# A hybrid linear-attention and sliding-window layer on one core: query/key projection by channels, and three sets of PE transposes given to DMA transposes

## What is computed

```python
h = rmsnorm(x, g_pre) * (1 + scale) + shift
gq, gk, gv, gg, ga, sq, sk, sv, sg = split(h @ w_in)
# linear attention (GLA): 4 heads, dk 64, dv 128, a forget gate per channel
log_a = log_sigmoid(ga @ w_alpha + b_alpha) / 16
S_t = exp(log_a) * S_(t-1) + k_t^T v_t ;  o_gla = (q_t * 64**-0.5) S_t
o_gla = rmsnorm(o_gla, gla_norm_g) * silu(gg)
# sliding window (SWA): 8 query heads, 2 key heads, hd 64, chunks of 64 tokens,
# own chunk and the one before, partial rotary, a learned sink per head
o_swa = sink_attention(rope(sq), rope(sk), sv) * silu(sg)
y = x + gate * rmsnorm(concat(o_gla, o_swa) @ w_out, g_post)
```

## Time and profile before

| | before |
| --- | --- |
| median of 3 runs | 1677.62 us |
| profiled run | 1677.3 us |
| its span, first to last instruction | 1675.6 us |
| busy PE, DVE, ACT, POOL | 1604.8, 1001.4, 659.0, 413.8 us |
| PE busy in a tile of 46.65 us in the middle | 46.65 us |
| mean granted PE clock | 0.979 |
| DMA, mean over the span | 71 GB/s |

### The profile page before, as it was taken

The page is one execution under the profiler, slowest core; times in us unless marked ns, Lnnn a source line. Parts: engine busy times, 40 slices in busy tenths (PEclk is TensorE's granted clock), DMA queues, the critical chain, the costliest instruction groups (busy, mean ns, idle before and its releaser), DMA issues.

```text
span 1675.6 us, 30638 instructions
## 1 busy us (share of the span) xinstructions
PE 1604.8 (96%) x12203; PEld 947.3 (57%) x12203; DVE 1001.4 (60%) x1711; ACT 659.0 (39%) x1983; POOL 413.8 (25%) x439
## 2 busy tenths in 40 slices
PE   8277999999999999999999999999999999999996
PEld 3135665555666666565566666556566666655553
DVE  1257665556666666655666666655656666655554
ACT  0254443443443434443444344444343433434432
POOL 0111222222222222222222222222222222222221
PEclk9679999999999999999999999999999999999998
DMA  8944322111122222121212222212112222221302
GB/s 271 296 120 102 90 64 64 50 50 38 50 63 63 63 63 63 56 57 37 51 50 63 63 63 63 63 50 51 37 55 58 63 63 63 63 63 45 79 18 61
DMA packets 199047, 119.13 MB, mean 71 GB/s; under 512 B 147005, under 2 KB 186438, under 8 KB 199014
## 3 DMA queue, kind: packets, MB, share of 16 engines
q1 hardware_dynamic: 189574, 115.51, 25.1%
q10 hardware_dynamic: 9440, 3.17, 0.9%
HBM read 49.23 MB, written 17.59 MB: 40 GB/s over the span
## 4 chain that ended last, share of the span: by engine, by line
PE 89%; DVE 2%; issue 1%; DMA 1%; ACT 1%; POOL 0%; ACTq 0%; SPq 0%; POOLq 0%
PE bank L446 55%; PE pairP L446 21%; PE pairQ L629 2%; PE bank L539 2%; PE bank L535 2%; PE bank L559 2%; PE pairP L582 1%; PE pairQ L546 1%; PE pairQ L603 1%; PE bank L570 1%; DMA hT<-h_tok 1%; PE bank L596 1%; PE bank L641 1%; PE pairQ L607 0%; PE bank L637 0%
## 5 line engine op out<-in xcount | busy, mean ns | idle before, releaser
L446 PE MATMUL bank<-w_hi,hT 128*128 128x512 f16 (+1 forms) x2640 | 751.1, 361 | 30.9 <-DMA hT<-h_tok 30.8
L446 PE MATMUL bank<-w_lo,hT 128*128 128x512 f16 (+1 forms) x1320 | 475.9, 361 | 0.0
L446 PEld LDWEIGHTS bank<-w_hi,hT 128*128 128x128 f16 x2640 | 259.0, 98 | 288.5 <-DMA hT<-h_tok 31.1
L446 PE MATMUL pairP<-wo_hi,late 128*128 128x512 f16 x1056 | 321.7, 381 | 2.5 <-DVE late L1025 2.5
L446 PE MATMUL pairP<-wo_lo,late 128*128 128x512 f16 x528 | 201.2, 381 | 0.0
L446 PEld LDWEIGHTS bank<-w_lo,hT 128*128 128x128 f16 x1320 | 129.7, 98 | 114.7 <-issue 1.9
L446 PE MATMUL bank<-hT,w_hi 128*128 128x128 f16 x2112 | 183.5, 221 | 3.2 <-DVE w_lo L913 3.2
L446 PE MATMUL bank<-hT,w_lo 128*128 128x128 f16 x1056 | 181.1, 221 | 0.0
L446 PEld LDWEIGHTS pairP<-wo_hi,late 128*128 128x128 f16 x1056 | 104.0, 99 | 125.0 <-DVE late L1025 2.9
L1172 POOL TENSOR_TENSOR xs<-xs,shift_row 128x1024 f32<-128x1024 f32 x33 | 79.7, 2414 | 374.2 <-DVE xs L929 374.2
L446 PEld LDWEIGHTS bank<-hT,w_hi 128*128 128x128 f16 x2112 | 162.7, 99 | 5.4 <-issue 3.3
(11 more groups left out here) (212 smaller groups left out, 2250.0 us busy)
## 6 DMA issues: line engine op xcount, KB each, us to landing
x_res<-x_in SPq DMA_DIRECT2D x33, 512.0 KB, 3.5
x_in<-in_x_prompt SPq DMA_DIRECT2D x32, 512.0 KB, 3.1
out<-stage SPq DMA_DIRECT2D x32, 512.0 KB, 2.7
w_hi<-in_w_ada SPq DMA_DIRECT2D x5, 1024.0 KB, 9.3
w_lo<-in_w_ada SPq DMA_DIRECT2D x5, 1024.0 KB, 13.1
wo_lo<-in_w_in SPq DMA_DIRECT2D x5, 1024.0 KB, 11.8
wo_hi<-in_w_in SPq DMA_DIRECT2D x3, 1024.0 KB, 11.2
stage<-in_w_ada SPq DMA_DIRECT2D x2, 1024.0 KB, 11.6
```

The costliest lines, as they stand in the source:

```text
L446: last = pe.matmul(out, a(c, i), b(c, j), start=(c == 0 and n == 0), stop=(c == KC - 1 and n == 2))
```

## The change

Three things are changed. The QK projection is made by channels, like the sg projection: four outputs [128 channels, 128 tokens], 24 matmuls each with 128 moving columns, so ACT's copy to `etmp` and the four transposes of line 570 are gone; DVE's products read bank4 directly and descale there. The mixed GLA rows are split in token-major form, high half by ACT and low half by DVE, into `m_tok`, which lies in the first half of `xs`; SP turns them by one DMA transpose into `mixT`, whose order is now slice, then half; the four transposes of line 582 are gone, and `x_scaled` waits for the transpose. The q and k pairs are turned by three DMA transposes (`transpose_qk`: two of 64 partitions for q, one for k straight into `kB`), issued by SP in every tile but tile 0, where ACT issues them; the twelve transposes of lines 603 and 607, ACT's copy to `qT` and DVE's copies from PSUM are gone, DVE copies half of `kB` into `kA` after the products with the decay. New waits: PE's output projection on `mT_loaded`, PE's scores on `qT_loaded`, SP on `mg_lo` and `pair_lo`, ACT on `mix_gla` ahead of its copies of the key and value projection.

```diff
@@ -146,11 +146,12 @@
...
         swa_ch = lambda a: a.rearrange("p (j k) -> p j k", j=KC // 2)
-        mixT = late[:, D:2 * D].bitcast(F16).rearrange("p (s c k) -> p s c k", s=2, c=KC)
+        mixT = late[:, D:2 * D].bitcast(F16).rearrange("p (c s k) -> p c s k", s=2, c=KC)
         x_in = sb("x_in", [P, 2, D])
...
         xs = sb("xs", [P, D])
+        m_tok = xs[:, 0:GH * DV].bitcast(F16).rearrange("p (c s k) -> p c s k", s=2, c=GH)
         hT = sb("hT", [P, 2, 2, KC, P], F16)
@@ -160,6 +161,7 @@
...
         qT = sb("qT", [P, 2, HEADS, CHUNK], F16)
+        q_tok_hb = qk_tok[:, 0:4, :].rearrange("p b (g k) -> p g b k", g=KVH)
         kA = sb("kA", [P, KVH, 2, P], F16)
@@ -170,12 +172,11 @@
...
         etmp = sb("etmp", [P, 512])
-        q_pair = etmp[:, :].bitcast(F16).rearrange("p (h s k) -> p h s k", h=HEADS, s=2)
+        q_pair = etmp[:, :].bitcast(F16).rearrange("p (g b s k) -> p g b s k", g=KVH, b=4, s=2)
         cache_k_tok = x_res[0:CHUNK, 0:P]
...
         cache_rows = cache_k_tok.rearrange("p (h k) -> p h k", h=KVH).unsqueeze(2).to_broadcast([CHUNK, KVH, 2, HD])
-        heads_tok = qk_tok[:, :, :].rearrange("p b (g k) -> p (b g) k", g=2)
-        k_twice = heads_tok[:, 8:10, :].unsqueeze(2).to_broadcast([P, KVH, 2, HD])
+        k_twice = qk_tok[:, 4, :].rearrange("p (g k) -> p g k", g=2).unsqueeze(2).to_broadcast([P, KVH, 2, HD])
         lsp = sb("lsp", [P, 2, P])
@@ -241,9 +242,6 @@
...
         gaT_ps = bank5[:, :].bitcast(F16)[0:2 * LOWRANK, 0:P]
-        pair16 = pairQ[:, :].bitcast(F16)
-        q_pair_ps = pair16[:, 0:HEADS * P].rearrange("p (h k) -> p h k", h=HEADS)
-        k_pair_ps = pair16[:, HEADS * P:(HEADS + 4) * P].rearrange("p (h s k) -> p h s k", h=KVH, s=2)
         cache_ps = bank4[:, :].bitcast(F16)[:, 0:4 * CHUNK].rearrange("p (h s k) -> p h s k", h=KVH, s=2)
...
@@ -273,6 +271,8 @@
...
         hT_loaded = [ctx.enter_context(nc.semaphore(f"hT_loaded{i}")) for i in range(2)]
+        mT_loaded = ctx.enter_context(nc.semaphore("mT_loaded"))
+        qT_loaded = ctx.enter_context(nc.semaphore("qT_loaded"))
         pT_loaded = ctx.enter_context(nc.semaphore("pT_loaded"))
@@ -301,6 +301,14 @@
...
             return w[:, :, at:at + HD]
+
+        def transpose_qk(eng):
+
+            for ch in range(2):
+                eng.dma_start_transpose(qT[:, ch, :, :], q_pair[CHUNK * ch:CHUNK * (ch + 1)].rearrange("p g b s k -> p (g b s k)"))\
+                   .then_inc(qT_loaded, 16)
+            eng.dma_start_transpose(kB[:, :, :, :].rearrange("p g s k -> p (g s) k"),
+                                    k_pair.rearrange("p g s d k -> p (g s d k)")).then_inc(qT_loaded, 16)
 
@@ -383,6 +391,19 @@
...
                         sp.dma_start(row_chunks(row[:, :]), mod_row(n, 1)).then_inc(scale_loaded[1], 16)
+                if c.prev:
+                    sp.wait_ge(sem["mg_lo"], c.t)
+                    sp.wait_ge(sem["pv_mm"], c.t)
+                    sp.wait_ge(pT_loaded, 16)
+                    sp.sem_inc(sem["mT_go"], 1)
+                    sp.dma_start_transpose(mixT[:, 0:GH, :, :].rearrange("p c s k -> p (c s) k"),
+                                           m_tok.rearrange("p c s k -> p (c s k)")).then_inc(mT_loaded, 16)
+                if c.cur and not c.first:
+                    sp.wait_ge(sem["pair_lo"], c.t + 1)
+                    sp.wait_ge(sem["ka_prev"], c.t + 1)
+                    sp.wait_ge(pT_loaded, 16)
+                    sp.sem_inc(sem["qT_go"], 1)
+                    transpose_qk(sp)
                 if c.next and not c.first:
@@ -513,13 +534,22 @@
...
 
+                def project_channels(out, first, done):
+
+                    for b in range(4):
+                        col = first + P * b
+                        last = split_product(out[:, b, :], lambda cc, i: (w_hi, w_lo)[i][:, cc, col:col + P], h)
+                    last.then_inc(done, 1)
+
                 if c.cur:
...
                         pe.wait_ge(sem["at_d"], t)
-                    project(bank4, 512, W_QK, sem["qk_mm"])
+                    if c.first:
+                        pe.wait_ge(w_split, in_units_before[W_QK])
+                    project_channels(qk_ch, W_QK, sem["qk_mm"])
                     if c.first:
@@ -565,22 +595,9 @@
...
                     project(bank7, 512, W_SQ, sem["sq_mm"])
-                    pe.wait_ge(sem["qk_ev"], t + 1)
-                    for b in range(4):
-                        last = pe.transpose(qk_ch[:, b, :], etmp[:, b * P:(b + 1) * P], ident[:, :])
-                    last.then_inc(sem["qkt_mm"], 1)
                     pe.wait_ge(sem["ksg_ev"], t + 1)
...
                     pe.transpose(gaT_ps, ga_pair[:, :], ident16[:, :]).then_inc(sem["gat_mm"], 1)
-                if c.prev:
-                    pe.wait_ge(sem["mix_gla"], t)
-                    if c.second:
-                        pe.wait_ge(sem["modt_ev"], 2)
-                    else:
-                        pe.wait_ge(sem["y_mul"], t - 1)
-                    for cc in range(GH):
-                        last = pe.transpose(pairP_c[:, cc, :], gates[:, cc * P:(cc + 1) * P], ident[:, :])
-                    last.then_inc(sem["mixt_mm"], 1)
                 if c.cur:
@@ -596,22 +613,17 @@
...
                     last.then_inc(sem["z_mm"], 1)
-                    pe.wait_ge(sem["pair_lo"], t + 1)
-                    if c.prev:
-                        pe.wait_ge(sem["s_upd"], t)
-                    for head in range(HEADS):
-                        last = pe.transpose(q_pair_ps[:, head, :], q_pair[:, 2 * (head % 4) + head // 4, :, :],
-                                            ident16[:, :])
-                    for g in range(KVH):
-                        for part in range(2):
-                            last = pe.transpose(k_pair_ps[:, g, part, :], k_pair[:, g, part, :, :], ident16[:, :])
-                    last.then_inc(sem["qks_mm"], 1)
                 if c.prev:
                     pe.wait_ge(sem["mixt_lo"], t)
+                    pe.wait_ge(mT_loaded, 16 * t)
+                    if c.second:
+                        pe.wait_ge(sem["modt_ev"], 2)
+                    else:
+                        pe.wait_ge(sem["y_mul"], t - 1)
                     for n in range(2):
...
                             pe.wait_ge(w_split, len(IN_UNITS) + (n + 1) * OUT_UNITS // 2)
-                        last = split_product(pairP[:, 512 * n:512 * (n + 1)], lambda cc, i: mixT[:, i, cc, :],
+                        last = split_product(pairP[:, 512 * n:512 * (n + 1)], lambda cc, i: mixT[:, cc, i, :],
                                              lambda cc, i: (wo_hi, wo_lo)[i][:, cc, 512 * n:512 * (n + 1)])
@@ -619,8 +631,10 @@
...
                     mod_to_rows(2 * KC, 3 * KC, 2)
-                pe.wait_ge(sem["qks_ev"], t + 1)
+                pe.wait_ge(qT_loaded, 48 * (t + 1))
                 pe.wait_ge(sem["k_ev"], t + 1)
+                if c.prev:
+                    pe.wait_ge(sem["s_upd"], t)
                 for ch in range(2):
@@ -646,10 +660,7 @@
...
                     pe.wait_ge(w_split, in_units_before[W_SG])
-                for j in range(KC // 2):
-                    col = W_SG + P * j
-                    last = split_product(bank6[:, P * j:P * (j + 1)], lambda cc, i: (w_hi, w_lo)[i][:, cc, col:col + P], h)
-                last.then_inc(sem["sg_mm"], 1)
+                project_channels(swa_ch(bank6[:, :]), W_SG, sem["sg_mm"])
 
@@ -750,12 +761,15 @@
...
                     rsqrt_of(o_r[:, :], o_ln[:, :], o_ss[:, :], DV, sem["o_lnd"], sem["o_rs"], t)
+                if c.prev:
+                    act.wait_ge(sem["mix_gla"], t)
+                    act.activation(m_tok[:, :, 0, :], swa_ch(gates[:, 0:512]), ACT.Copy).then_inc(sem["mg_hi"], 1)
                 if c.cur:
...
                     if c.prev:
-                        act.wait_ge(sem["qks_mm"], t)
+                        act.wait_ge(qT_loaded, 48 * t)
                     if c.sample:
@@ -766,10 +780,6 @@
...
                        .then_inc(sem["ksg_ev"], 1)
-                    if c.prev:
-                        act.wait_ge(sem["sg_g"], t)
-                    act.wait_ge(sem["qk_mm"], t + 1)
-                    act.activation(etmp[:, :], bank4[:, :], ACT.Copy, scale=DESCALE).then_inc(sem["qk_ev"], 1)
                     act.wait_ge(sem["sq_mm"], t + 1)
@@ -785,14 +795,14 @@
...
                 if c.prev:
-                    act.wait_ge(sem["mixt_mm"], t)
-                    act.activation(mixT[:, 0, 0:GH, :], pairP_c[:, 0:GH, :], ACT.Copy)
                     act.wait_ge(sem["mix_swa"], t)
-                    act.activation(mixT[:, 0, GH:KC, :], swa_ch(gates[:, 512:1024]), ACT.Copy).then_inc(sem["mixt_hi"], 1)
+                    act.activation(mixT[:, GH:KC, 0, :], swa_ch(gates[:, 512:1024]), ACT.Copy).then_inc(sem["mixt_hi"], 1)
                 if c.cur:
                     act.wait_ge(sem["rope"], t + 1)
-                    act.wait_ge(sem["qkt_mm"], t + 1)
```

(39 more changed lines are left out.)

6 lines of the change are left out of this document (3 added, 3 removed).

## The result

The changed kernel is slower: 1761.49 us median (4 runs, 1757.87 to 1761.87) against 1677.57 for the kernel before, a ratio of 1.0493 (95% interval 1.0479 to 1.0507). The forecast was 1643.4, range 1630 to 1655. The profiled execution took 1757.87 us; its span is 1756.1, 80.5 more than before.

A forecast was written before the change was run, and what follows sets the result against it. The prediction took TensorE (PE) as the limit in steady tiles, 46.72 us each. Profiled run 1677.3 - 46.8 (31 tiles x 1.51) + 12.6 for first and last tiles = 1643.1, set to the median: 1643.4 us, range 1630 to 1655.

The forecast's parts named there:

- The steady tile: Tiles 2 to 32: PE work removed less work added saves 1.51 us a tile (1.42 to 1.68), 46.8 us over 31.
- The QK exchange: QK projection: four f32 transposes go (0.44 us), 96 matmuls of 128 columns replace 24 of 512 (0.29 us dearer).
- the removal of the other sixteen transposes: PE, steady tile: transposes of GLA rows (0.59 us), q pairs (0.55) and k pairs (0.22) leave the chain.
- The transfers hide in steady tiles: Steady tiles: new DMA transposes land before PE needs them, GLA rows over 6 us spare, q/k 5; cost nothing.
- late copies: Rival, 5%: the copy into kA comes late by about a microsecond in every tile; 1675 us.
- transposes in series: Rival, 5%: the three q/k transposes land one after the other, 4.2 us each, 2.0 us stall a tile; 1706 us.
- the exchange: Rival, 2%: QK's 96 matmuls cost 69 ns each, 6.6 us, leaving 0.4 us gain a tile; 1678 us.
- The ends: First two tiles and last one: new waits cost 12.6 us in all (8 to 17).
- Tile 0: ACT's three q/k transpose issues delay the squares of the next x to 119.4: +4.3 us (2.5 to 6.8).
- Tile 1: Output projection waits for the GLA transpose queued on SP, then runs at a lower clock: +7.1 us (5 to 8.5).
- the last tile: Tile 33: output projection waits for the low half and the transpose's landing: +1.2 us (0.5 to 1.9).
- PE's loop body no longer stays on the engine: Rival, 3%: PE's grown loop is fetched at each of 14 turns, 4.2 us each, 59 us; 1702 us.

The follow-up runs named there:

- experiment 3: Changed kernel with the QK projection token-major again (ACT's copy and four f32 transposes back), DMA transposes kept: 1654.07 us.
- Experiment 1: Changed kernel with PE's loop written out, all 34 tiles one behind the other without a jump back (the written-out kernel): 1649.69 us.
- the edit that undoes the order: Written-out changed kernel, with ACT issuing tile 0's q/k transposes behind its decay exponentials instead of ahead of the next x's squares: 1643.12 us.
- experiment 5: Kernel before with the channel-major QK projection only, plus 24 PE transposes (48 instructions) into an unused bank ahead of tile 0: 1730.54 us.
- the kernel with 78 transposes: Changed kernel, loop kept, with 78 PE transposes (156 instructions) into an unused bank ahead of tile 0: 1726.22 us.
- both kernels with one wait a jump: The kernel of experiment 5 (1730.54 us) and the kernel with 78 transposes (1726.22 us).
- all eight kernels with a loop: Before; token-major QK; channel QK alone, also with 24 transposes; changed, also with 48, 78, or 12 transposes and two first-tile edits: 1640.6 to 1761.5 us.

## Why the prediction was wrong

**The steady tile was right in kind, a tenth too large in size.** Forecast 1.51 us a tile (1.42 to 1.68), measured 46.72 - 45.37 = 1.35, below the lower bound. The QK exchange alone gave 0.20 where the step had 0.44 - 0.29 = 0.15; 57 ns a matmul held: half of the 10.83 us piece is 5.41. Too large was the removal of the other sixteen transposes: 1.14 by experiment 3, not 1.36. The chain shows the 0.22: the V projection, which now follows one single transpose, takes 5.29 where it took 5.18 behind the transposes of line 582, and the output projection 10.47 behind the decay matmuls where it took 10.36 behind line 607. The V projection in the chain of before, right behind line 582:

```profile
817.92 5.18 PE bank L446 x24
```

So each of these two pieces costs 0.11 us more without the transposes in front of it: what a transpose takes in the chain is not all given back when it goes. Why is not shown; four decay matmuls in front don't do the same. With the 0.05 that the exchange gave beyond its step, 1.51 - 1.35 = 0.16 is missing in a tile, 5.0 us over 31.

**The transfers hide in steady tiles: right.** SP's issues in the changed kernel, in the tile without the stop, and DVE's copy into kA:

```profile
913.43 1.24 SPq L399 DMA_TRANSPOSE late<-xs  x1
923.75 2.51 SPq L308 DMA_TRANSPOSE qT<-etmp  x2
926.31 1.26 SPq L310 DMA_TRANSPOSE kB<-junk  x1
933.68 1.84 SPq L413 DMA_TRANSPOSE hT<-h_tok  x1
```

```profile
929.03 1.93 DVE L1093 COPY kA<-kB 128x256 f16<-128x256 f16 x1
```

POOL's addition of the shift at that time, and the landing of the GLA rows (median):

```profile
928.52 2.35 POOL L1186 TENSOR_TENSOR xs<-xs,shift_row 128x1024 f32<-128x1024 f32 x1 [7.19 <-DVE xs L940]
```

```profile
late<-xs SPq DMA_TRANSPOSE x33, 2.7
```

The small transposes issue in 1.24 to 1.26 us each (forecast 1.14 and 0.79, bounds 0.43 and 1.85); by the trace's list of DMA issues they land in 2.5 to 2.7 us, not 3.5. The GLA rows are there by 916.1, PE takes them at 923.84; kA is ready at 930.96 and the scores begin at 934.31, 3.4 us later, where 5 were forecast at the middle price. Not the landing took the difference but the copy: the step put it at 0.2 us, and it took 1.93, where a copy of the same shape at line 1054 takes 0.22. It ended 0.09 us behind POOL's addition of the shift. In all 32 tiles with that addition the copy takes 1.06 to 1.94 and ends 0.07 to 0.09 behind it; in tile 32, which has none, it takes 0.23. So the copy is held until POOL is done, and the step had no such term. Experiment 1 settles it: 45.37 us in each tile, without the time that the jumps gave. So the rivals "late copies" and "transposes in series" fall, and with 5.41 us for 96 matmuls "the exchange" too.

**The ends: 14.3 us at the start, not 11.4, and 0.1 at the end, not 1.2** (0.1 is the -1.3 above and the 1.35 of one tile, which the forecast counts among its 31). Tile 0: the squares at 119.92, forecast 119.4 (a shift of 4.81, forecast 4.3); the edit that undoes the order starts them at 113.59, 6.53 sooner than in the written-out kernel, and gave 6.6: the chain held, one for one. Tile 1: the output projection started at 182.02, forecast 179.2. The step took SP's queue as shifted by tile 0's 4.3; x_res was issued at 174.31, 7.3 later than before, because the output weights ahead of it had slipped as well (SP's last issue for them at 171.32, 164.06 before), and the load of x behind it waited for its copy. The forecast had the right instruction in front of the transpose and didn't follow what delays that one. The projection took 12.55 - 11.09 = 1.46 longer, forecast 1.6, at a granted clock of 0.84 against 0.94: PE had been idle for 12.1 us ahead of it, and its clock was 0.50 (1.2 GHz) over the last 7. In the last tile the output projection starts 3.63 us after the state update (1731.74 in its chain), 2.99 before: +0.64, and takes 12.43, not 12.73.

Without the jumps these steps would have come out at 1643.4 + 5.0 + 2.9 - 1.1 = 1650.2; the written-out kernel measured 1649.7. The working of the forecast was 6 us off, inside its range, for a kernel that keeps its code at hand.

**The step that failed is the loop.** It stood among the rivals: "PE's loop body no longer stays on the engine", 3%, 1702, with the packets named as its sign. The forecast asked how much PE work goes and whether each transfer lands in time; whether PE's own instructions are there in time it left to this rival. The mechanism was named, its price was too small and its chance had no support. The argument against it was that 22 packets "show none of it at today's size". They show that the loop of before stayed; they say nothing of how near it was to the limit, and the step had just worked out that the body grows by a seventh. With no row that shows a limit, the growth was the fact at hand. It was a matter of place as well: 24 instructions further on, the same loop has no such wait, which no row of before could tell. The price was 14 x 4.2. It is 13 jumps, not 14, and 8.31 us each, not 4.2: two waits, 3.90 and 2.62 in the jump shown, by the reading of experiment 5 because the loop began just ahead of a boundary, and the slower clock after them (0.50, then 0.58): the 96 matmuls took 0.82 + 6.45 = 7.27 us, not 5.41, another 1.86. By the list of waits a jump waited 79.7 / 13 = 6.13 on average, which leaves 2.2, most of it the clock's.

Open: what sets the price of one fetch. It was 3.90, 2.62, 3.2 on average in experiment 5 and 3.9 in the kernel with 78 transposes. The transpose of the probabilities runs at that time (its median landing went from 4.3 to 5.2 in the changed kernel, and is 4.3 in the written-out one and in both kernels with one wait a jump); whether code and transposes hold each other up was not tried.

## What to carry to other kernels

Before adding instructions to an engine's loop, count them, and after the change compare the packets of the instruction queue: if they rose by a multiple of the jumps back, the loop is fetched again at each, and the price sits in "issue" waits at the first instructions of a turn. Such a loss need have nothing to do with what the edit is for: write the loop out, or move it by a few harmless instructions, before judging the change. The transfers that took over PE's work hid where PE was the limit; look for the price of such transfers in the first tiles, in the program order of the queue that issues it and of everything that delays this queue.

## What the hardware showed beyond that

- A loop of 1746 PE instructions turned without a fetch and one of 1682 did not: what counts in all eight kernels with a loop is the number of 256-instruction blocks touched, seven or eight. 24 instructions ahead of the loop were worth 111 us.
- Reading 28098 PE instructions straight on (109 packets) cost nothing: 45.37 us a tile, as with the loop.
- DMA transposes of 1024 columns on 64 or 128 partitions, and of 512 columns, all issue in about 1.25 us in a steady tile and land in 2.5 to 2.7 (medians); 2048 columns take 1.85 and 4.2.
- Around the two waits of 3.90 and 2.62 us PE's granted clock went from 1.00 (2.4 GHz) to 0.50 (1.2 GHz) and was back at 1.00 in the last 3.23 us of QK; the 96 matmuls took 1.86 us longer for it.
- A DVE copy of 128x256 f16 within SBUF that began during a POOL addition ended 0.07 to 0.09 us after it, 32 times of 32, and took up to 1.94 us; without the addition it took 0.23.
